# First modulation sums in column groups, index scores by pairs of heads, index sums read between selection rounds

## What is computed

```python
c_act = jax.nn.silu(c)                          # 1 x 1024
mod = c_act @ w_ada[l] + b_ada[l]               # 1024 x 6144
sh1, sc1, gt1, sh2, sc2, gt2 = jnp.split(mod, N_MOD, axis=-1)
h = modulate(rms_norm(x, g_mix[l]), sh1, sc1)   # x * (1 + scale) + shift
proj = h @ w_in
```

```python
def block(args):                                # 128 queries
    rel = jax.nn.relu(jnp.einsum('bqhd,bsd->bqhs', qi, k_idx))   # 8 heads, d = 64
    score = jnp.einsum('bqh,bqhs->bqs', wi, rel)
    score = jnp.where(key_pos[None, None, :] <= t[None, :, None], score, NEG)
    _, sel = lax.top_k(score, top_k)            # top_k = 128
    ...                                         # attention over the selected keys
```

## Time and profile before

| | us |
|---|---|
| median of 3 runs | 2013.96 |
| lowest and highest | 2011.36, 2021.73 |
| the profiled execution, device time | 2014.79 |
| its span | 2012.9 |
| TensorE busy | 1929.9 |
| VectorE busy | 1021.9 |
| ScalarE busy | 661.9 |
| GpSimd busy | 242.9 |

### The profile page before, as it was taken

The page is one execution under the profiler, slowest core; times in us unless marked ns, Lnnn a source line. Parts: engine busy times, 40 slices in busy tenths (PEclk is TensorE's granted clock), DMA queues, the critical chain, the costliest instruction groups (busy, mean ns, idle before and its releaser), DMA issues.

```text
span 2012.9 us, 23871 instructions
## 1 busy us (share of the span) xinstructions
PE 1929.9 (96%) x8989; PEld 1340.2 (67%) x8989; DVE 1021.9 (51%) x1877; ACT 661.9 (33%) x1238; POOL 242.9 (12%) x241
## 2 busy tenths in 40 slices
PE   7999899996899999989999999999999999999998
PEld 3478576673233334456788888888667878888886
DVE  6474545344233322774565555555347756455554
ACT  2572722241111113367322222232336632222222
POOL 1000000024354520213200000020000020000001
PEclk9999999997899999989999999999989999999999
DMA  9555134357999896011222322323340022322201
GB/s 327 195 135 193 60 127 166 137 191 259 412 407 391 312 356 238 24 42 42 84 84 97 112 84 89 120 84 125 134 157 1 1 84 84 104 106 84 97 29 42
DMA packets 106024, 292.58 MB, mean 145 GB/s; under 512 B 14553, under 2 KB 25535, under 8 KB 92864
## 3 DMA queue, kind: packets, MB, share of 16 engines
q1 hardware_dynamic: 92352, 266.60, 35.8%
q0 software_dynamic: 12560, 22.30, 3.5%
q10 hardware_dynamic: 1008, 2.29, 0.3%
HBM read 331.22 MB, written 24.69 MB: 177 GB/s over the span
## 4 chain that ended last, share of the span: by engine, by line
PE 87%; DVE 7%; DMA 2%; issue 2%; ACT 1%; ACTq 0%; DVEq 0%; POOL 0%; SPq 0%; POOLq 0%
PE bank L1430 18%; PE bank L1432 18%; PE bank L1431 18%; PE bank L1827 9%; PE bank L1347 5%; PE bank L1853 4%; PE bank L1389 3%; PE bank L1415 2%; PE bank L1401 2%; PE bank L1883 1%; PE bank L1634 1%; DVE top L3347 1%; PE bank L1421 1%; DVE hT L3348 1%; PE bank L1375 1%
## 5 line engine op out<-in xcount | busy, mean ns | idle before, releaser
L3237 DVE TENSOR_TENSOR weights_low<-weight_ring,weights_high 128x1024 fp32r<-128x1024 f32 x128 | 160.0, 1250 | 265.9 <-ACT weights_high L2309 265.9
L1432 PE MATMUL bank<-hidden_high,weights_low 128*128 128x512 f32 x688 | 267.6, 389 | 0.0
L1430 PE MATMUL bank<-hidden_high,weights_high 128*128 128x512 f32 x624 | 242.7, 389 | 0.0
L1431 PE MATMUL bank<-hidden_low,weights_high 128*128 128x512 f32 x624 | 242.7, 389 | 0.0
L2309 ACT ACTIVATE weights_high<-weight_ring 128x1024 fp32r<-128x1024 f32 x128 | 135.6, 1059 | 325.6 <-PE bank L1432 325.6
L1430 PE MATMUL bank<-normed_high,weights_high 128*128 128x512 f32 x512 | 200.4, 391 | 2.4 <-DVE weights_low L3237 2.4
L1431 PE MATMUL bank<-normed_low,weights_high 128*128 128x512 f32 x512 | 199.3, 389 | 0.0
L1432 PE MATMUL bank<-normed_high,weights_low 128*128 128x512 f32 x512 | 199.3, 389 | 0.0
L1827 PE MATMUL bank<-weight_ring,arena 128*64 128x512 f32 x464 | 177.4, 613 | 14.5 <-issue 9.4
L1185 POOL TENSOR_TENSOR chunk_mask<-small,probs_T 128x512 f32<-128x512 f32 x5 | 6.5, 1305 | 1173.7 <-ACT probs_T L2296 1173.7
L1432 PEld LDWEIGHTS bank<-hidden_high,weights_low 128*128 128x128 f32 x688 | 129.1, 188 | 26.8
(11 more groups left out here) (573 smaller groups left out, 3539.0 us busy)
## 6 DMA issues: line engine op xcount, KB each, us to landing
weight_ring<-in_w_up SPq DMA_DIRECT2D x16, 2048.0 KB, 8.7
weight_ring<-in_w_down SPq DMA_DIRECT2D x16, 2048.0 KB, 7.8
weight_ring<-in_w_gate SPq DMA_DIRECT2D x29, 1024.0 KB
weight_ring<-in_w_up SPq DMA_DIRECT2D x29, 1024.0 KB
weight_ring<-in_w_ada SPq DMA_DIRECT2D x12, 2048.0 KB, 12.7
weight_ring<-in_w_down SPq DMA_DIRECT2D x19, 1024.0 KB
hT<-in_w_down SPq DMA_DIRECT2D x19, 1024.0 KB
weight_ring<-in_w_in SPq DMA_DIRECT2D x7, 2048.0 KB, 14.7
```

The lines of the kernel that those rows point to most:

```text
L1430: pe.matmul(dst, high, rhs_high, start=first, stop=False)
L1431: pe.matmul(dst, high, rhs_low, start=False, stop=False)
L1432: return pe.matmul(dst, low, rhs_high, start=False, stop=last)
L3237: dve.tensor_tensor(piece_half(w_lo, ch, q), piece_of(ch, q), piece_half(w_hi, ch, q).bitcast(F32), ALU.subtract).then_inc(s_wlo, 1)
```

## The change

First, TensorE sums all four first chunks by itself (mod_quarter_sums). A new tile silu_spread, 128 x 8 x 32, is zero but for column 0 of each piece, which holds silu_c; it is cleared by VectorE at the start and filled by one ScalarE copy. Piece k = 4 half + n is multiplied into output partitions 32 n to 32 n + 31, so four column groups of the array take a piece each, in two halves: 8 matmuls of 128*32 x 512 a chunk. ScalarE copies the whole 128 x 512 bank to mod_acc (mod_sums_out), and mod_columns sums the partitions and turns. mod_row_sum, mod_row_turn and VectorE's part for these chunks are gone. The latents are placed differently between them, and ScalarE copies sum 0 ahead of the bias table. Second, index_scores issues the heads by pairs, two products, two products, and the sums two pairs behind. Third, the read of an index sum is a function of its own (index_sum_out) and stands between selection rounds: block 2's after 10 rounds of block 1, block 3's after 8 rounds of block 2. TOP_EARLY falls from 9 to 5, so last_top runs 11 rounds, ahead of steps 0 to 20.

```diff
-MOD_PE = (4, 4, 0, 0)
-MOD_DONE = tuple(sum(KD - k for k in MOD_PE[:n + 1]) for n in range(len(MOD_PE)))
...
-TOP_EARLY = 9
+TOP_EARLY = 5
...
-        mod_acc, c_in, mod_row = ar(14336, 2, T), ar(11392, P, rows=KD), ar(13312, 2, T, rows=1)
+        mod_acc, c_in, silu_spread = ar(14336, 2, T), ar(11392, P, rows=KD), ar(13312, KD, 32)
...
                 g = G[("mod", c)]
                 begin(g)
-                pe.wait_ge(s_macc, MOD_DONE[3] + KD * (n - 3))
+                if n < 4:
+                    g_read(pe, G[("mod_sum", c)])
+                else:
+                    pe.wait_ge(s_macc, KD * (n - 3))
...
-            def mod_row_sum(c, n, between=None):
+            def mod_quarter_sums(c):
...
-                for k in range(MOD_PE[n]):
-                    pe.matmul(psum(g)[0:1, :], silu_c[:, k:k + 1], w[:, k, :], start=(k == 0), stop=False)
-                if between is not None:
-                    between()
-                pe.wait_ge(s_macc, MOD_DONE[n])
-                pe.matmul(psum(g)[0:1, :], ones[:, 0:1], mod_acc[:, n % 2, :], start=(MOD_PE[n] == 0), stop=True)\
-                    .then_inc(mm_done, 1)
...
+                for half in range(2):
+                    for n in range(4):
+                        k = 4 * half + n
+                        last = pe.matmul(psum(g)[32 * n:32 * n + 32, :], silu_spread[:, k, :], w[:, k, :],
+                                         start=(half == 0), stop=(half == 1), skip_group_check=True)
                 last.then_inc(mm_done, 1)
...
-            mod_row_sum(MOD_FIRST[0], 0, bias_and_vectors)
-            mod_row_sum(MOD_FIRST[1], 1)
+            mod_quarter_sums(MOD_FIRST[0])
+            bias_and_vectors()
+            mod_quarter_sums(MOD_FIRST[1])
             for n in range(2):
-                mod_row_turn(MOD_FIRST[n], n)
+                mod_columns(MOD_FIRST[n], n)
...
+            latent(0, 0)
+            mod_quarter_sums(MOD_FIRST[2])
+            latent(0, 1)
+            mod_quarter_sums(MOD_FIRST[3])
+            mod_columns(MOD_FIRST[2], 2)
+            mod_columns(MOD_FIRST[3], 3)
+            latent(0, 2)
+            for m in range(3):
+                latent(1, m)
...
+                for pair in range(H // 2 + 2):
+                    if pair < H // 2:
+                        g = G[("idx", qt)] + 2 * pair
+                        for side in range(2):
+                            g_free(pe, g + side)
+                        for side in range(2):
+                            r = slice(64 * side, 64 * side + 64)
+                            pe.matmul(psum(g + side)[:, 0:n], q_idx[r, pair, qt * P:qt * P + P], kidx_n[r, 0, 0:n],
+                                      start=True, stop=True).then_inc(mm_done, 1)
+                    if pair >= 2:
+                        for i in (2 * pair - 4, 2 * pair - 3):
...
+            act.wait_ge(s_spread, 1)
+            act.activation(silu_spread[:, :, 0], silu_c[:, :], ACT.Copy).then_inc(s_cs, 1)
...
+            def mod_sums_out(n):
+                if n >= 2:
+                    act.wait_ge(mm_done, done(G[("mod", MOD_FIRST[n - 2])]))
+                evac(G[("mod_sum", MOD_FIRST[n])], mod_acc[:, n % 2, :])
...
-            mod_partial(MOD_FIRST[0], 0, MOD_PE[0], KD)
...
-            top_rounds(1, 0, TOPK // 8)
-            top_rounds(2, 0, TOPK // 8)
+            index_sum_out(1)
+            top_rounds(1, 0, 10)
+            index_sum_out(2)
+            top_rounds(1, 10, TOPK // 8)
+            top_rounds(2, 0, 8)
+            index_sum_out(3)
+            top_rounds(2, 8, TOPK // 8)
             top_rounds(3, 0, TOP_EARLY)
```

117 lines of the change are left out of this document (45 added, 72 removed).

## The result

The changed kernel takes 1993.95 us (median of 4 runs, 1987.59 to 1998.31), the kernel before beside it 2014.8. The ratio of the two is 0.9891 [0.9869, 0.9913]; the medians are 20.9 us apart. Timed again twice on other chips it gave 0.9902 [0.9882, 0.9923] and 0.9899 [0.9878, 0.9921], with medians of 1995.84 and 1996.47. The two later medians lie just inside it. The profiled execution took 1987.59 us (span 1985.7), the fastest of its four.

What follows compares the result with a forecast made beforehand. TensorE, busy 96% of the span, was taken as the bound, with VectorE setting the DSA start. 2014.8 less 6.5 (start) and 7.3 (index stage) gave 2001.0, less 0.8 to the median: 2000.2 us, range 1995.5 to 2008.0.

Steps and rivals of the forecast that it cites:

- gain of the start: Start up to the small key projection: sums on TensorE and the new latent order save 6.5 us (4.2 to 8.8).
- (a): Index stage on VectorE: the first read of an index sum moves 2.5 us earlier (0.9 to 2.9).
- (c): DSA steps 14 to 20: four moved selection rounds return, mostly in VectorE's idle time; 1.2 us sticks out (0 to 6).
- gain of the index stage: Index stage on VectorE: earlier first read, four rounds off the path, some returning later; 7.3 us saved (0.9 to 8.9).
- The third and fourth chunk: Start: these weights land at about 31.1 and 36.5, before TensorE wants them, the fourth by 2.6 us.
- second slow stretch: Start, latents behind the 1.37 us gap: with the gap covered, the slow stretch goes too, saving 1.8 us.
- (1): DSA steps: the moved rounds pace the steps, so they cost 6 us instead of 1.2; 2005.0 us, chance 0.15.
- (2): Start: the second slow stretch stays, with its 1.8 us; 2002.0 us, chance 0.12.
- (3): Index stage: the pairs of heads don't overlap and only the alternation is saved; 2002 us, chance 0.05.
- (4): DSA steps: the halved clock lasts until the projections near 947; 2035 us, chance 0.05 with whatever else is slower.
- I take a gain at either place as kept to the end: Whole kernel: gains at the start and index stage last, since semaphores tie all later work to TensorE.
- the edges of both places: Spread of the two gains: 4.2 to 8.8 us at the start, 0.9 to 8.9 at the index stage.

Runs made afterwards that it cites:

- e3: Changed kernel with the first halves of the latents ordered as before (two, sum 2, the third, sum 3, columns): 1999.45 us, ratio 0.9919.
- e5: Changed kernel with nine of block 3's selection rounds ahead of step 0, as before, instead of five: 2000.24 us, ratio 0.9919.
- a0: The kernel before, unchanged, timed again for a second profile: 2015.21 us, ratio 1.0000.
- e7: Kernel before with only the selection rounds moved, five of block 3's ahead of step 0 instead of nine: 2014.94 us, ratio 0.9997.
- e12: Kernel before with each index score a product of all 128 rows instead of 64: 2012.09 us, ratio 0.9978.
- The two halves alone: Changed kernel with the index stage and selection as before, 2006.48 us; kernel before with only the index part of the change, 2006.22 us.
- e10: Changed kernel with index scores head by head as before, but each a product of all 128 rows: 1994.87 us, ratio 0.9901.
- e14: Kernel before with the first two turns of the modulation rows repeated five more times, padding TensorE's matmul count: executed once, 2026.76 us.

## Why the prediction was nearly right and where it fell short

**Held.** The three profiles of the changed kernel beside the first of the kernel before, in us:

| | forecast | measured |
|---|---|---|
| a sum in four column groups | 1.92 | 1.92 |
| first sum to first latent | 8.35 | 8.10, 8.00, 8.00 |
| gain of the start, from the first sum | 6.5 | 8.6, 7.2, 7.1 |
| block 3 on TensorE | 11.0 | 11.0 |
| TensorE at the DSA steps, on the scale of before | 865 | 864.8 |
| (a) first read sooner | 2.5 | 2.9 |
| VectorE's first score sooner | 8.5 | 8.7 |
| (c) rounds that stick out in the steps | 1.2 | 1.0 |
| gain of the index stage | 7.3 | 7.7, 7.7, 8.5 |

The third and fourth chunk came in time, and there was no second slow stretch without its gap (e3). The 1.0 of (c) is partly luck: with nine rounds early (e5) the steps are 1.0 us shorter than in the kernel before, for a reason that stays open, so the four moved rounds cost 2.0. The rivals fell: (1) by (c) and e5, (2) and (3) by the rows above, (4) by the changed kernel's stretches behind the wait,

```profile
860.00:870.00 10.00, 8.39 (x32) 6.91 (x33) 6.69 (x30) 7.48 (x34) 0.72 (x1) 0.51 0.01 2
880.00:890.00 10.00, 8.79 (x53) 6.00 (x51) 8.50 (x28) 7.54 (x26) 4.99 (x5) 1.00 0.00 1
```

where the halved clock lasts to about 870, in the steps of 128 keys, as in the earlier trace rows.

**The step that failed** is term (a) of the index stage, the first read that "I take -2.5", together with the base it was taken from: "2014.8 - 6.5 - 7.3 ... for an execution like the profiled one, which lies 0.8 above the median". The one profile had block 1 at full clock, and the prediction put the clock there at nothing, though it asked after the clock at the start and in the steps (rival 4). In executions with the fall, a0 and e7, the first read stands 17.0 us behind the block's start, against 7.8 in the changed kernel: there the term is 9.2 us and not 2.5 to 2.9, and 5.7 of the difference last to behind the DSA steps. The median holds this in about half of the executions, which adds some 2.7 us (e12, with the width given above) that stood in no row the forecast was made from. That the profiled execution lay near the median all the same is chance: it was without the fall, but behind the DSA steps it was 2.5 us slower than a0.

**The second miss** is "I take a gain at either place as kept to the end", with no term for what else could move. At the 2144 KB load the shorter wait brought 1.0 to 1.6 us, and the half-clock stretch of 1.3 to 1.6 that four of five profiles show behind the longer one stayed out, some 1.1 on the mean: 2.1 to 2.7 together.

With both, 7.1 to 8.6, 7.7 to 8.5, 2.7 and 2.1 to 2.7 make 19.6 to 22.5, where 22.0, 19.7 and 20.4 were measured (one less the ratio, times the time before beside it; by the medians 20.9, 17.3 and 21.2). The two halves alone, 7.5 and 8.5, are each lower than these terms make them (9.2 to 11.3 and 10.4 to 11.2), though their intervals reach that far, so the sum is not confirmed that way. The range was too narrow at its lower end for the same reason. It took the edges of both places whole: 2014.8 - 0.8 - 8.8 - 8.9 = 1996.3, and 1 us of spread. Even if every edge had come true it could not have reached 1993.95, since it had nothing for block 1's clock and nothing for the rest of the program. Some of what was right was right for the wrong reason: of the 10.8 us by which the pairs bring TensorE sooner to the steps, the overlap makes 5.5, and it could have been left out at a cost of 0.8 to 1.6 in the profiles and none in the times (e10).

## What to carry to other kernels

Take two or three profiles of the kernel before, not one, and compare the granted clock stretch by stretch before a sum is made against one of them: a time equal to the median doesn't make an execution a typical one. Where matmuls on part of the rows alternate with full ones and the clock falls there in some profiles, as in block 1 here, group them, even if the overlap itself saves little. And move work off one engine only as far as the other's head start reaches: the same four rounds were worth 4 us behind earlier scores and 0.5 without them.

## What the runs showed of the hardware that was not expected

- TensorE's clock fell to its lower level with the engine busy 14.87 of 15.00 us, on 64-row products of 256 columns alternating with full ones, in three of six profiles of kernels with that order; never in twelve profiles with the same products by pairs, nor in two with full rows.
- It was at the lower level on very small products too. e14 makes 48 turns of one column in a row, 17.02 us for them, and runs at 0.50 into the latents behind, of which 8 take 10.09 us:

```profile
30.85 17.02 PE L1465 MATMUL bank<-ones,arena 1*128 1x1 f32 x96
49.33 10.09 PE L1635 MATMUL bank<-hT,arena 128*128 128x512 f32 x16 [1.46 <-ACT hT L2402]
```

```profile
35.00:50.00 15.00, 13.54 (x62) 13.29 (x62) 2.15 (x6) 1.63 (x3) 1.56 (x2) 0.50 0.62 199
```

- A 2144 KB load takes 9.1 to 9.4 us in the five profiles in which one 0.02 MB transfer of the instruction queue falls into it, and 7.8 to 8.4 in the other fifteen. Twenty matmuls more at the program's start decide whether it does so at 1400 us.
- Behind TensorE's wait for that load the clock fell in four of five profiles where the wait was 3.2 to 3.5 us, and in none of fifteen where it was 1.9 to 2.5.
